# The S5 mixer of a four-layer backbone: chunks stored by step in the block, and the injection computed with tokens as the stationary side

## The chip, the cores and the metric

One core of a Trainium2 chip runs the whole program. The metric is the device time of one execution in microseconds (us); lower is better. The engines of the core are named as in the profile: PE (TensorE matmuls), PEld (its weight loads), DVE (VectorE), ACT (ScalarE), POOL (GpSimd) and SP, which only issues DMAs here. A difference of about 0.2% (4.4 us) is what a measurement of this kernel can tell from none.

## The reference

A backbone of four layers over 256 latent tokens and 256 context tokens of width 1024, all in float32. Each layer has a token mixer (latent attention, Hyena, S5, FNet, in that order) and a gated feed-forward part; both are normed and modulated. The change is in the S5 mixer of layer 2, cut here to what it computes:

```python
def s5_scan(u, lam_bar, b_bar, h0, reverse):
    bu = jnp.einsum('bngc,gsc->bngs', u.astype(jnp.complex64), b_bar)
    a = jnp.broadcast_to(lam_bar, bu.shape)
    a_cum, xs = lax.associative_scan(_lin_rec, (a, bu), axis=1, reverse=reverse)
    if h0 is None:
        return xs
    return xs + a_cum * h0[:, None]

# s5_mixer, for each direction (forward, backward), 64 groups of 16 channels, 64 complex states
xs_ctx = s5_scan(u_ctx, lam_bar, b_bar, None, reverse)
h0 = xs_ctx[:, 0] if reverse else xs_ctx[:, -1]
xs_lat = s5_scan(u_lat, lam_bar, b_bar, h0, reverse)
y_lat = y_lat + jnp.einsum('bngs,gcs->bngc', xs_lat, c_mat).real.reshape(B, L, D)
# after both: y = a * sigmoid(b) with (a, b) = gelu(y_lat) @ w_glu + b_glu
```

A linear recurrence runs over the context and then over the latent tokens, in either direction; only the latent tokens have an output.

## The kernel before

**How S5 is staged.** Each stream of 256 tokens is 32 chunks (`CH`) of 8 tokens (`STEP`), and 8 chunks are a block (`BLK`); context and latents together are 64 chunks, 8 blocks (`blocks`). The join that ends layer 1 writes the modulated tokens into `h_split` (L693) by step in the chunk, then chunk. 32 small DMAs (`tokens`, L2253; half from SP's queue, half from POOL's) bring them to `u`: partitions are 16 channels times 8 steps, and each of the 64 groups has 64 columns, its chunks.

**Injection.** `S5.tensor` has 16 rounds `n` (`NB`) of four groups. For every group and each of the real and imaginary parts (`i`) a matmul takes a 128x128 weight `et` as the stationary side and streams the group's 64 columns of `u` past it (L2475), into one bank; two banks (`INJECT`) alternate. ACT moves a bank into `e` with three copies (L2521 is a helper's line, that of every copy in `S5.scalar`): partitions 0 to 63 hold the states of the forward direction, 64 to 127 those of the backward one, which are written in reverse order. `e` is stored by group, part, step in the block and then block, so one step of all 8 blocks is 8 elements in a row.

**Recurrence.** On DVE, `inside` (L2375 to L2378) runs the seven steps within all blocks, four operations a step; `across` (L2385 to L2388) runs over the ends of the 8 blocks, 28 operations on 64 elements; `carries` (L2430 to L2433) adds to each step what the block before left. It is done for groups 0 to 31 (in two parts) and then 32 to 63. The `carries` of the first half run on POOL, those of the second on DVE, which waits for POOL first since both use `t0`.

**States to output.** `forward` and `backward` copy the states before each chunk from `e` to `s2` (on ACT, but for the second half's `backward`, which is DVE's). Meanwhile PE has computed the part within a chunk (L2489, weights `m0`). Then PE adds the states' part (L2502, weights `f`, once for each half), turns the result (L2513), and after the skip (L2412) and the Gelu comes the gated projection `Gated` (L864), whose result DVE multiplies (L2417).

**Order.** Every engine's program is written out by hand, stage after stage, and runs in order; semaphores join them. Two things are slotted in. The modulation vectors of later layers are computed in ticks (`mods`, L397: eight 32-row matmuls each, on 1 MB of weights that a `refill` on SP's queue brings, L360); `place` says how many ticks a stage does and how early the next loads may be issued. Every fourth tick ends a vector, which ACT copies (L408), PE turns (L374) and DVE stores (L418). SP issues in this order for S5: four `et` loads of 1 MB, the table of powers, two refills, the tokens, two refills, eight loads of `m0`, four more of `et`, eight of `f`.

## Time and profile before

| | us |
|---|---|
| time, median of 3 runs | 2223.07 |
| fastest and slowest of them | 2221.59, 2223.78 |
| the profiled execution's own time | 2222.09 |
| its span | 2220.3 |
| PE busy in it | 2089.5 (94%) |
| DVE, ACT, POOL busy | 1163.3, 865.4, 157.9 |
| S5's first injection matmul (L2475) starts at | 1547.08 |
| its last matmuls on the states (second L2502) start at | 1644.11 |

The page gives busy times and shares, the span in 40 slices, and the costliest groups. The 1.8 us between the span and the execution's time lie outside of the traced instructions. PE is busy nearly all of the time, so a stage matters by how long PE takes for it or is kept waiting in it. S5 stands at 1547 to 1716; in the page's 29th and 30th slice (each 55.5 us) the granted clock of PE falls to 0.5 and 0.7 of full speed, which is 2.4 GHz.

### The profile page before, as it was taken

The numbers are of one execution on the slowest core, as the hardware profiler recorded it, in microseconds if no ns is written. First come the engines' busy times: TensorE is split into PE (matmuls) and PEld (weight loads), VectorE is DVE, ScalarE is ACT, GpSimd is POOL, SyncE is SP. The second block draws the span as 40 slices with busy tenths as digits, with TensorE's granted clock in tenths as the row PEclk, the third lists the DMA queues.
The fourth block names the chain that finished last, engine by engine and source line by source line (L and its number), as shares of the span: only waits on it lengthen the run. The fifth ranks groups of instructions, "written<-read, shape, count | busy, mean of one in ns | idle before, by whom it ended". The sixth has DMA issues, their size and how long they took to land.

```text
span 2220.3 us, 31627 instructions
## 1 busy us (share of the span) xinstructions
PE 2089.5 (94%) x13233; PEld 1641.6 (74%) x13233; DVE 1163.3 (52%) x1961; ACT 865.4 (39%) x1416; POOL 157.9 (7%) x225
## 2 busy tenths in 40 slices
PE   4999999999999989999999999997959999898998
PEld 2756567777777767766468878875947899788997
DVE  2332552655666566647164665755661645526454
ACT  2442334433333453231253333344632544515444
POOL 0000110102101100010010210111200000000000
PEclk8999999999999999999999999998579999999999
DMA  6335341545535546442153443444584555314553
GB/s 258 133 111 183 133 152 42 197 147 172 178 119 187 180 172 216 165 135 103 57 170 106 130 136 100 141 134 162 233 305 145 190 189 175 123 58 153 189 184 102
DMA packets 227243, 342.14 MB, mean 154 GB/s; under 512 B 9590, under 2 KB 190625, under 8 KB 224860
## 3 DMA queue, kind: packets, MB, share of 16 engines
q1 hardware_dynamic: 216064, 310.27, 40.8%
q0 software_dynamic: 10320, 29.58, 4.6%
q8 instruction: 105, 1.72, 0.3%
q10 hardware_dynamic: 716, 0.26, 0.0%
q14 instruction: 38, 0.31, 0.0%
HBM read 317.66 MB, written 24.51 MB: 154 GB/s over the span
## 4 chain that ended last, share of the span: by engine, by line
PE 87%; DVE 7%; ACT 2%; DMA 2%; issue 1%; SPq 0%; POOL 0%; ACTq 0%; DVEq 0%
PE bank L956 21%; PE bank L957 20%; PE bank L958 20%; PE bank L819 4%; PE bank L397 3%; PE bank L864 3%; PE bank L2475 2%; PE bank L1724 1%; PE bank L1351 1%; PE bank L637 1%; DMA arena<-mod_w 1%; PE bank L2057 1%; PE bank L627 1%; PE bank L495 1%; DVE arena L710 1%; DVE arena L721 1%
## 5 line engine op out<-in xcount | busy, mean ns | idle before, releaser
L956 PE MATMUL bank<-h_hi,w_hi 128*128 128x512 f32 (+1 forms) x1480 | 512.0, 346 | 11.8 <-DVE h_lo L725 11.2
L957 PE MATMUL bank<-h_lo,w_hi 128*128 128x512 f32 (+1 forms) x1480 | 504.4, 341 | 0.0
L958 PE MATMUL bank<-h_hi,w_lo 128*128 128x512 f32 (+1 forms) x1480 | 504.4, 341 | 0.0
L917 DVE TENSOR_TENSOR w_lo<-ring,w_hi 128x1024 fp32r<-128x1024 f32 (+1 forms) x282 | 323.8, 1185 | 284.6 <-ACT w_hi L910 284.5
L956 PEld LDWEIGHTS bank<-h_hi,w_hi 128*128 128x128 f32 x1480 | 283.0, 191 | 50.8 <-DVE h_lo L725 15.3
L910 ACT ACTIVATE w_hi<-ring 128x1024 fp32r<-128x1024 f32 (+1 forms) x282 | 274.0, 1019 | 102.0 <-PE bank L958 100.2
L958 PEld LDWEIGHTS bank<-h_hi,w_lo 128*128 128x128 f32 x1480 | 283.0, 191 | 32.0 <-issue 0.2
L957 PEld LDWEIGHTS bank<-h_lo,w_hi 128*128 128x128 f32 x1480 | 283.3, 191 | 29.2 <-issue 0.2
L956 PE MATMUL bank<-g_hi,w_hi 128*128 128x512 f32 (+1 forms) x704 | 241.1, 342 | 0.0
L957 PE MATMUL bank<-g_lo,w_hi 128*128 128x512 f32 (+1 forms) x704 | 236.9, 337 | 0.0
L958 PE MATMUL bank<-g_hi,w_lo 128*128 128x512 f32 (+1 forms) x704 | 236.7, 336 | 0.0
L956 PEld LDWEIGHTS bank<-g_hi,w_hi 128*128 128x128 f32 x704 | 133.5, 190 | 22.7 <-issue 8.7
L958 PEld LDWEIGHTS bank<-g_hi,w_lo 128*128 128x128 f32 x704 | 133.5, 190 | 14.3
L957 PEld LDWEIGHTS bank<-g_lo,w_hi 128*128 128x128 f32 x704 | 133.6, 190 | 12.9
L1076 ACT ACTIVATE g_hi<-arena 128x512 fp32r<-128x512 f32 (+1 forms) x88 | 45.9, 525 | 234.4 <-DVE arena L1101 234.4
L1070 ACT ACTIVATE arena<-bank 128x512 f32<-128x512 f32 (+1 forms) x88 | 42.8, 491 | 190.3 <-PE bank L958 188.6
L397 PE MATMUL bank<-mod_ring,silu_c 128*32 128x256 f32 x1408 | 94.1, 392 | 24.2 <-DMA mod_ring<-mod_w 24.1
L1101 DVE TENSOR_TENSOR arena<-arena,bank 128x512 f32<-128x512 f32 (+1 forms) x88 | 48.2, 551 | 112.4 <-PE bank L958 110.5
L397 PEld LDWEIGHTS bank<-mod_ring,silu_c 128*32 128x32 f32 x1408 | 39.5, 111 | 63.7 <-DMA mod_ring<-mod_w 29.2
L956 PE MATMUL bank<-h_hi,hy_w_hi 128*128 128x512 f32 x192 | 76.4, 398 | 0.8 <-DVE h_lo L725 0.7
L957 PE MATMUL bank<-h_lo,hy_w_hi 128*128 128x512 f32 x192 | 74.9, 390 | 0.0
L958 PE MATMUL bank<-h_hi,hy_w_lo 128*128 128x512 f32 x192 | 74.8, 390 | 0.0
(328 smaller groups left out, 2959.7 us busy)
## 6 DMA issues: line engine op xcount, KB each, us to landing
ring<-ffn_w SPq DMA_DIRECT2D x120, 1024.0 KB, 5.1
mod_ring<-mod_w SPq DMA_DIRECT2D x88, 1024.0 KB, 6.8
ring<-ffn_w SPq DMA_DIRECT2D x16, 768.0 KB, 4.6
ring<-hy_w_in SPq DMA_DIRECT2D x12, 1024.0 KB, 5.3
arena<-mod_w SPq DMA_DIRECT2D x8, 1024.0 KB, 17.3
s_in_weights<-arena POOLq DMA_DIRECT2D x32, 256.0 KB, 3.3
s_out_weights<-arena POOLq DMA_DIRECT2D x16, 512.0 KB, 3.4
arena<-s_in_weights SPq DMA_DIRECT2D x8, 1024.0 KB, 10.9
```

The costliest lines, as they stand in the source:

```text
L397: last = nc.tensor.matmul(MODB[32 * g:32 * g + 32, 0:256], silu_c[:, k, :], self.slot(m)[:, kk, 256 * g:256 * g + 256], start=(k == 0), st ...
L819: last = nc.tensor.matmul(self.banks[c % 4][:, 0:self.n], v[:, kl, q * P:(q + 1) * P], self.rhs(k), start=(k == 0), stop=(k == self.kk - 1))
L864: last = nc.tensor.matmul(self.bank(c, t)[:, 0:self.n], v[:, k, q * P:(q + 1) * P], self.rhs(k), start=(k == 0), stop=(k == KD - 1))
L910: nc.scalar.activation(self.hi[:, i % SPLIT, a:b], self.w.slot(i)[:, a:b], ACT.Copy).then_inc(w_rounded, 1)
L917: last = unit.tensor_tensor(self.lo[:, i % SPLIT, c:c + w], self.w.slot(i)[:, c:c + w], self.hi[:, i % SPLIT, c:c + w].bitcast(F32), ALU.s ...
L956: nc.tensor.matmul(o, w[0], v[0], start=first, stop=False)
L957: nc.tensor.matmul(o, w[0], v[1], start=False, stop=False)
L958: return nc.tensor.matmul(o, w[1], v[0], start=False, stop=last)
L1070: nc.scalar.activation(self.silus[:, q, 0:n], self.out(i, q)[:, 0:n], ACT.Silu).then_inc(ffn_silu, 1)
L1076: nc.scalar.activation(g_hi[:, c + q, 0:n], self.silus[:, q, 0:n], ACT.Copy).then_inc(ffn_g_rounded, 1)
L1101: nc.vector.tensor_tensor(self.silus[:, q, 0:n], self.silus[:, q, 0:n], self.out(i, q)[:, 0:n], ALU.mult).then_inc(ffn_product, 1)
L2475: last = nc.tensor.matmul(bank[self.INJECT[n % 2]][:, o:o + 2 * CH], self.et[:, c % 4, 4 * (n % 2) + gb, i, :], self.u[:, 4 * n + gb, :], ...
```

## The change

**Layout.** The tokens are written to `h_split` with a chunk's place as step in the block first, then block, and with context and latents exchanged, so that context comes first. `e` becomes group, part, stream (context or latents, `a`), step in the block `q`, block `b` (four to a stream). One step of a stream is a run of four elements, and a group's part is a run of 64 in the order in which it leaves the bank. `ends` is a small area of its own for the ends of the blocks before each latent block.

**Injection.** A round has four matmuls: a group's 64 columns of `u` are the stationary side and the 256 columns of `et` (both parts) stream; two groups go to partitions 0 to 63 and 64 to 127 of the bank (`inject`). The bank is copied to SBUF (`move_injected`: DVE for rounds 0 to 3, ACT after), four PE transposes turn it so that states are partitions (`turn_states`, banks `STATES`), and ACT copies it to `e` with two copies. A round's turn is issued behind the next round's matmuls.

**Recurrence.** `across` of the first half moves from DVE to POOL, ahead of `carries`; each `carries` gets two small copies to `ends`. POOL now also waits until all rounds are in `e`.

**Queues and ticks.** The two refills ahead of the tokens on SP's queue are gone, the last four `et` loads come right behind the tokens, and two modulation ticks leave the join of layer 1; `states` has four in place of two, `scan` two in place of four, and the join in the middle of layer 3 has two in place of none. The multiplication at the end (L2417) becomes four operations a column block.

```diff
-                if self.fills:
+                if self.fills == 2:
                     mods.tensor(pe, (self, 1))
...
                         if self.split:
-                            src = src.rearrange("p (m s) -> p m s", s=STEP)
-                            dst = h_split[:, :, k, a // LAT, :].rearrange("p s m -> p m s")
+
+                            src = src.rearrange("p (b q s) -> p b q s", q=BLK, s=STEP)
+                            dst = h_split[:, :, k, 1 - a // LAT, :].rearrange("p s (q b) -> p b q s", q=BLK)
...
-            SCAN = [4 * (BLK - 1) * n + 4 * (2 * CH // BLK - 1) + c for n, c in ((2, 0), (1, 8))]
+            ACROSS, CARRIES = 4 * (2 * CH // BLK - 1), 10
+            SCAN = [4 * (BLK - 1) * 2, 4 * (BLK - 1) + ACROSS + CARRIES]
...
+                pool.wait_ge(self.e_moved, 2 * self.NB)
...
-                self.carries(nc.gpsimd, slice(0, 32), self.t0, self.raw.rearrange("p i s g -> p (i s g)"), then)
+                gs = slice(0, 32)
+                self.across(nc.gpsimd, gs, self.t0[:, 0:64], self.t0[:, 64:128], (self.signed[:, 0], self.signed[:, 1]), then)
+                self.carries(nc.gpsimd, gs, self.t0, self.raw.rearrange("p i s g -> p (i s g)"), then)
...
-                self.e = area(4096, GROUPS, 2, STEP, 2 * CH // BLK)
+                self.e = area(4096, 2 * GROUPS, 2 * CH).rearrange("p (g r) (a q b) -> p g r a q b", r=2, a=2, q=BLK)
...
+                self.ends = area(29184, GROUPS, 2, 4)
...
+                self.rows = self.t0.rearrange("p (a n) -> p a n", a=2)
...
-                mods.place((self, "turn"), 0)
-                mods.place((self, "states"), 2, p0 + 0.3)
-                mods.place((self, "scan"), 4, p0 + 0.4)
+                mods.place((self, "states"), 4, p0 + 0.4)
+                mods.place((self, "scan"), 2, p0 + 0.4)
                 mods.place((self, "turns"), 2, p0 + RING)
...
-                mods.refill(sp, p0 + 0.1)
                 for qt in range(4):
                     self.tokens(sp, 0, qt)
+                for c in range(4, 8):
+                    inject(c)
                 mods.refill(sp, p0 + 0.2)
...
                 for c in range(8):
                     toeplitz(c)
-                for c in range(4, 8):
-                    inject(c)
-                sp.wait_ge(self.e_summed, self.NB)
+                sp.wait_ge(self.e_summed, self.injected(self.NB - 1))
...
+                for n in range(2):
+                    self.move_injected(dve, V.tensor_copy, n)
...
+                for a in range(2):
+                    V.tensor_copy(self.signed[:, a], self.lab[:, 2 + a, 0:32]).then_inc(self.placed, 1)
+                for n in range(2, 4):
+                    self.move_injected(dve, V.tensor_copy, n)
...
-                    wide = lambda a: self.lab[:, a, gs].unsqueeze(3).to_broadcast([P, gs.stop - gs.start, 2, blocks])
-                    ta, tb = (v[:, 0:(gs.stop - gs.start) * 2 * blocks].rearrange("p (g r b) -> p g r b", r=2, b=blocks) for v in (self.scaled, self.t1))
+                    n = gs.stop - gs.start
+                    wide = lambda a: self.lab[:, a, gs].unsqueeze(3).unsqueeze(4).to_broadcast([P, n, 2, 2, blocks // 2])
+                    ta, tb = (v[:, 0:n * 2 * blocks].rearrange("p (g r a b) -> p g r a b", r=2, a=2, b=blocks // 2) for v in (self.scaled, self.t1))
                     for i in range(1, BLK):
-                        prev, cur = self.e[:, gs, :, i - 1, :], self.e[:, gs, :, i, :]
+                        prev, cur = self.e[:, gs, :, :, i - 1, :], self.e[:, gs, :, :, i, :]
                         scan(V.tensor_tensor(ta, wide(0), prev, ALU.mult), False)
...
-                        dve.wait_ge(self.e_moved, 3 * gs.stop // 4)
+                        dve.wait_ge(self.e_moved, 2 * gs.stop // 4)
...
-                        if gs.start == 0:
-                            mods.vector(dve, (self, "turn"))
-                    across(slice(32 * hf, 32 * hf + 32))
-                dve.wait_ge(self.carried, 8)
+                gs = slice(32, 64)
+                self.across(V, gs, self.scaled[:, 0:64], self.t1[:, 0:64], (self.lab[:, 2, gs], self.lab[:, 3, gs]), scan)
+                dve.wait_ge(self.carried, self.ACROSS + self.CARRIES)
...
+                    order = lambda v: v.rearrange("p (s q b) -> p b s q", s=STEP, q=BLK)
+                    dst = Y[:, c, 0:LAT].rearrange("p (b q s) -> p b s q", q=BLK, s=STEP)
+                    src, gate = order(self.up.bank(c, 0)[:, 0:LAT]), order(self.sig[:, c % 2, :])
+                    for b in range(CH // BLK):
+                        last = V.scalar_tensor_tensor(dst[:, b], src[:, b], vcol("s5_b_glu", c), gate[:, b], ALU.add, ALU.mult)
+                    last.then_inc(self.glu, 1)
...
+            def across(self, unit, gs, ta, tb, factors, scan):
+
+                ends = self.e[:, gs, :, :, BLK - 1, :]
+                ta, tb = (v.rearrange("p (g r) -> p g r", r=2) for v in (ta, tb))
+                for b in range(1, 2 * CH // BLK):
+                    prev, cur = ends[:, :, :, (b - 1) // 4, (b - 1) % 4], ends[:, :, :, b // 4, b % 4]
+                    scan(unit.tensor_tensor(ta, factors[0], prev, ALU.mult), False)
+                    scan(unit.tensor_tensor(tb[:, :, ::-1], factors[1], prev, ALU.mult))
+                    scan(unit.tensor_tensor(ta, ta, tb, ALU.add))
+                    scan(unit.tensor_tensor(cur, cur, ta, ALU.add))
...
+                scan(unit.tensor_copy(self.ends[:, gs, :, 0:1], self.e[:, gs, :, 0, nq, 3:4]), False)
+                scan(unit.tensor_copy(self.ends[:, gs, :, 1:4], self.e[:, gs, :, 1, nq, 0:3]))
                 tq = [self.tab[:, i, 0:nq, gs].rearrange("p q g -> p g q").unsqueeze(3).to_broadcast([P, n, nq, 4]) for i in range(2)]
-                end = [self.e[:, gs, r, nq, 3:7].unsqueeze(2).to_broadcast([P, n, nq, 4]) for r in range(2)]
+                end = [self.ends[:, gs, r, :].unsqueeze(2).to_broadcast([P, n, nq, 4]) for r in range(2)]
```
```diff
-                dst, src = self.states(slice(0, STATE), hf)
-                copy(dst[:, :, :, 0], src[:, :, 3:7, BLK - 1]).then_inc(done, 1)
-                copy(dst[:, :, :, 1:BLK], src[:, :, 4:8, 0:BLK - 1]).then_inc(done, 1)
+                dst, ends, src = self.states(slice(0, STATE), hf)
+                copy(dst[:, :, 0:4], ends).then_inc(done, 1)
+                copy(dst[:, :, 4:CH], src).then_inc(done, 1)
...
+            INJECT, STATES, OUT, TURNED = (0, 1), (4, 5), (0, 1, 4, 5), ((0, 1), (4, 5))
...
+                if n >= 2:
+                    pe.wait_ge(self.placed, self.moved(n - 2))
+                for p in range(2):
+                    for z in range(2):
+                        gb = 2 * p + z
+                        last = nc.tensor.matmul(bank[self.INJECT[n % 2]][64 * z:64 * z + 64, 256 * p:256 * p + 256], self.u[:, 4 * n + gb, :],
+                                                self.et[:, c % 4, 4 * (n % 2) + gb].rearrange("p i n -> p (i n)"), start=True, stop=True)
+                last.then_inc(self.e_summed, 1)
+
+            def move_injected(self, eng, copy, n):
+                eng.wait_ge(self.e_summed, self.injected(n))
+                if n >= 2:
+                    eng.wait_ge(self.e_summed, self.turned(n - 2))
+                copy(self.rows[:, n % 2], bank[self.INJECT[n % 2]][:, :]).then_inc(self.placed, 1)
+
+            def turn_states(self, pe, n):
+
+                pe.wait_ge(self.placed, self.moved(n))
+                if n >= 2:
+                    pe.wait_ge(self.e_moved, 2 * (n - 1))
+                dst = bank[self.STATES[n % 2]][:, :].rearrange("p (a z i j) -> p a i z j", a=2, z=2, i=2)
+                for p in range(2):
+                    for i in range(2):
+                        o = 256 * p + P * i
+                        last = nc.tensor.transpose(dst[:, p, i], self.rows[:, n % 2, o:o + P], ident[:, :])
+                last.then_inc(self.e_summed, 1)
...
+                for n in range(self.NB + 1):
+                    if n < self.NB:
+                        self.inject(pe, n)
+                    if n:
+                        self.turn_states(pe, n - 1)
...
-                    act.wait_ge(self.e_summed, n + 1)
-                    src = bank[self.INJECT[n % 2]][:, :].rearrange("p (g b q) -> p g b q", g=8, q=BLK)
-                    dst = self.e[:, 4 * n:4 * n + 4].rearrange("p g r q b -> p (g r) b q")
-
-                    copy(dst[0:STATE, :, 4:8], src[0:STATE, :, 0:4]).then_inc(self.e_moved, 1)
-                    copy(dst[0:STATE, :, 0:4], src[0:STATE, :, 4:8]).then_inc(self.e_moved, 1)
-                    copy(dst[STATE:P, :, ::-1, ::-1], src[STATE:P]).then_inc(self.e_moved, 1)
-                act.wait_ge(self.carried, 8)
+                    if n == 3:
+                        act.wait_ge(self.placed, self.moved(3))
+                    if 3 <= n < self.NB - 1:
+                        self.move_injected(act, copy, n + 1)
+                    act.wait_ge(self.e_summed, self.turned(n))
+
+                    src = bank[self.STATES[n % 2]][:, :].rearrange("p (a m) -> p a m", m=CH)
+                    dst = self.e[:, 4 * n:4 * n + 4].rearrange("p g r a q b -> p (g r a) (q b)")
+                    copy(dst[0:STATE], src[0:STATE]).then_inc(self.e_moved, 1)
+                    copy(dst[STATE:P, :, ::-1], src[STATE:P]).then_inc(self.e_moved, 1)
+                mods.scalar(act, (self, "states"))
+                act.wait_ge(self.carried, self.ACROSS + self.CARRIES)
...
-                for key in ("turn", "states", "scan"):
-                    mods.scalar(act, (self, key))
+                mods.scalar(act, (self, "scan"))
...
-            if l == 2:
-                mid.place_mods((2, 0))
+            else:
+                mid.place_mods((2,))
             ffn = Ffn(l, n_out, mid, post, TICKS[l])
             if l == 0:
                 post.place_mods()
             if l == 1:
-                post.place_mods((2, 2), (len(panels) + 0.1, len(panels) + 0.2))
+                post.place_mods((2, 0), (len(panels) + 0.2, None))
             if l == 2:
-                post.place_mods((2, 0))
+                post.place_mods((2,))
```

PE, between the join of layer 1 (L495 spreads its norms) and the gated projection; `bank` is PSUM, `arena` the large SBUF area. Before:

```order
L495 MATMUL bank<-r_post,sel 128x128 x4
L495 MATMUL bank<-r_pre,sel 128x128 x4
L397 MATMUL bank<-mod_ring,silu_c 32x256 x16
L2475 MATMUL bank<-arena 128x64 x64
L374 MATMUL bank<-ident,mod_rows 128x128 x2
L2475 MATMUL bank<-arena 128x64 x64
L2489 MATMUL bank<-arena 32x128 x64
L397 MATMUL bank<-mod_ring,silu_c 32x256 x16
L2502 MATMUL bank<-arena,tail 32x128 x64
L397 MATMUL bank<-mod_ring,silu_c 32x256 x16
L374 MATMUL bank<-ident,mod_rows 128x128 x2
```

Now, with `ring` holding the copied rows; the pair of four matmuls and four transposes stands 15 times, of which the rows show the first ones and the last:

```order
L495 MATMUL bank<-r_post,sel 128x128 x4
L495 MATMUL bank<-r_pre,sel 128x128 x4
L2505 MATMUL bank<-arena 64x256 x8
L2524 MATMUL bank<-ident,ring 128x2x64 x4
L2505 MATMUL bank<-arena 64x256 x4
...
L2524 MATMUL bank<-ident,ring 128x2x64 x8
L2542 MATMUL bank<-arena 32x128 x64
L397 MATMUL bank<-mod_ring,silu_c 32x256 x16
L374 MATMUL bank<-ident,mod_rows 128x128 x2
L397 MATMUL bank<-mod_ring,silu_c 32x256 x16
L2555 MATMUL bank<-arena,tail 32x128 x64
L397 MATMUL bank<-mod_ring,silu_c 32x256 x16
```

The 16 matmuls of ticks (L397) between L495 and the injection are gone, the 128 matmuls of 128x64 are 64 of 64x256 with 64 transposes between them, and the ticks stand behind L2542 (L2489 before). The line numbers are those of the changed kernel.

POOL, from its token DMAs on. Before:

```order
L2253 DMA arena<-h_sb 128x1x128 x16
L2430 TENSOR_TENSOR ring<-ring,arena 128x896
L2431 TENSOR_TENSOR ring<-ring,arena 128x896
L2432 TENSOR_TENSOR ring<-ring 128x896
L2433 TENSOR_TENSOR arena<-arena,ring 128x32x7x4
```

Now (the four operations on 64 elements stand seven times before the copies):

```order
L2256 DMA arena<-h_sb 128x1x128 x16
L2436 TENSOR_TENSOR ring<-ring,arena 128x64
L2437 TENSOR_TENSOR ring<-ring,arena 128x32x2
L2438 TENSOR_TENSOR ring<-ring 128x64
L2439 TENSOR_TENSOR arena<-arena,ring 128x64
...
L2444 COPY arena<-arena 128x64
L2445 COPY arena<-arena 128x64x3
L2451 TENSOR_TENSOR ring<-ring,arena 128x896
L2452 TENSOR_TENSOR ring<-ring,arena 128x896
L2453 TENSOR_TENSOR ring<-ring 128x896
L2454 TENSOR_TENSOR arena<-arena,ring 128x32x28
```

The 28 small operations of `across` and two copies stand ahead of the eight of `carries`.

## Rows read from the trace of the kernel before

**Rows 1.** The chain that ended last, in order of time: start us, us, what.

```profile
1537.35 9.69 DMA arena<-h_sb
1547.08 27.57 PE bank L2475 x128
1574.65 0.43 PE bank L374 x2
...
1604.69 0.70 DVE bank L2375
...
1624.12 0.27 DVE bank L2385
...
1631.43 1.09 DVE ring L2430
...
1640.20 3.82 ACT tail L2521 x2
1644.11 6.30 PE bank L2502 x128
1650.41 1.04 PE bank L2513 x8
...
1655.43 27.63 PE bank L864 x128
```

**Rows 2.** Groups by shape, 1545 to 1660 us; columns as in the page's part 5.

```profile
L2475 PEld LDWEIGHTS bank<-arena 128*128 128x128 f32 x256 | 54.8, 333 | 1.2 <-DMA arena<-h_sb 1.2
...
L2521 ACT ACTIVATE arena<-bank 64x512 f32<-64x512 f32 x16 | 17.9, 1116 | 0.4
...
L2521 ACT ACTIVATE tail<-arena 64x1792 f32<-64x1792 f32 x3 | 10.1, 3359 | 0.0
L2377 DVE TENSOR_TENSOR bank<-bank,ring 128x256 f32<-128x256 f32 x14 | 6.1, 432 | 0.5
...
L2521 ACT ACTIVATE arena<-bank 128x512 f32<-128x512 f32 x3 | 1.7, 584 | 2.8 <-PE bank L2502 2.8
```

**Rows 3.** Busy times by stretch; the last three are clock, DMA share, GB/s.

```profile
core 0: us, PE busy (x) PEld busy (x) DVE busy (x) ACT busy (x) POOL busy (x), PEclk, DMA share, GB/s
...
1566.00:1572.00 6.00, 6.00 (x30) 6.00 (x30) 5.62 (x15) 3.67 (x6) 0.00 (x0) 0.50 1.03 419
...
1606.00:1610.00 4.00, 3.03 (x80) 1.97 (x72) 3.85 (x6) 0.00 (x0) 3.92 (x3) 1.00 1.01 420
...
1630.00:1634.00 4.00, 1.51 (x18) 0.62 (x18) 3.79 (x9) 0.38 (x1) 0.00 (x0) 1.00 0.84 270
```

**Rows 4.** SP's queue in time: start us, us, what.

```profile
1526.65 1.25 SPq L360 DMA_DIRECT2D mod_ring<-mod_w  x2
```

**Rows 5.** PE in order of time, 1544 to 1630 us.

```profile
1544.87 1.94 PE L397 MATMUL bank<-mod_ring,silu_c 128*32 128x256 f32 x16 [3.69 <-DMA mod_ring<-mod_w]
...
1602.21 5.09 PE L2489 MATMUL bank<-arena 128*32 128x128 f32 x128
...
1622.06 5.40 PE L2502 MATMUL bank<-arena,tail 128*32 128x128 f32 x128 [13.03 <-ACT tail L2521]
```

**Rows 6.** DVE in order of time, the end of layer 1's join.

```profile
1543.49 0.69 DVE L721 TENSOR_TENSOR arena<-x_sb,bank 128x512 f32<-128x512 f32 x1
```

**Rows 7.** POOL in time, first and last of eight operations of `carries`.

```profile
1596.22 2.32 POOL L2430 TENSOR_TENSOR ring<-ring,arena 128x896 f32<-128x896 f32 x1 [46.24 <-DVE arena L2388]
...
1612.11 2.08 POOL L2433 TENSOR_TENSOR arena<-arena,ring 128x896 f32<-128x896 f32 x1
```

**Rows 8.** Groups by shape on POOL, the whole span.

```profile
L917 POOL TENSOR_TENSOR mla_o_lo<-ring,mla_o_hi 128x256 fp32r<-128x256 f32 x16 | 11.8, 771 | 247.2 <-ACT mla_o_hi L910 247.2
```

**Rows 9.** PE in order of time, between two shapes of tile, 1491 us.

```profile
1491.05 0.39 PE L958 MATMUL bank<-g_hi,w_lo 128*128 128x512 f32 x1
1491.36 0.43 PE L627 MATMUL bank<-arena,ones 128*32 128x128 f32 x8
```

**Rows 10.** All engines in order of time, the join inside layer 3.

```profile
2001.46 0.71 PE L495 MATMUL bank<-r_post,sel 64*128 64x128 f32 x4
...
2002.92 1.21 DVE L917 TENSOR_TENSOR w_lo<-ring,w_hi 128x1024 fp32r<-128x1024 f32 x1
```

84 lines of the change are left out of this document (34 added, 50 removed).

## The prediction

> **What bounds the kernel now.** I read the page first: PE is busy for 94% of the span, so the question for each stage is what PE does or waits for in it. Then the chain of waits through S5 [rows 1]. It goes through three things. PE's injection, two times 27.6 us for 64 matmuls each from 1547.08, with the turn of a modulation vector between them. Then DVE's recurrence on the second half of the groups, `inside` from 1604.69, `across` from 1624.12, `carries` from 1631.43. Then two ACT copies of 3.82 us at 1640.20, and PE's second run on the states at 1644.11. So 97.0 us lie between the first injection matmul and that run, and the injection is more than half of them.
>
> Why is the injection so slow? A matmul here takes 55.1/128 = 0.43 us for 64 columns (two records each, 0.215 us). The gated projection streams 256 columns with 0.216 us a record at the full clock [rows 1], which is about two cycles of 2.4 GHz a column, four for both records. The injection ran at half the clock, 0.50 [rows 3], and at 1.2 GHz four cycles for each of 64 columns would be 0.213 us, half of the measured 0.43. The other half is the weight load: PEld is busy for 54.8 us, as long as PE itself [rows 2]. PE was loading weights all the time.
>
> What stands ahead? The last tick before the injection waited 3.69 us for its weights and ran at 1544.87 [rows 5]; its 2 MB stand on SP's queue at 1526.65 [rows 4], ahead of the tokens, whose DMAs took 9.69 us [rows 1].
>
> **The start.** Two loads of 1 MB leave the head of the queue. At the 419 GB/s of a full stretch [rows 3] they are 2.1 MB / 419 = 5.0 us, and the ticks that waited for them are gone too. The first injection matmul can come at about 1542 in place of 1547. But the copy of its bank is DVE's now, and DVE's last work in the join begins at 1543.49 and takes 0.69 [rows 6]. So the start of the pipeline is DVE's, about 1544. DVE then does two copies (0.7 each, priced by its own operation on 512 elements in rows 6), the tables (16 operations) and two more, some 5.5 us; round 3 is turned after that and copied by ACT by 1553. That is an estimate; the bounds are 1552 and 1556.
>
> **A round of injection on PE.** Four matmuls stream 256 columns at four cycles, 4096 cycles in a row; if the two halves of the array, 64 columns of it each, work side by side, 2048: 1.71 us at 1.2 GHz, 0.85 at 2.4. No row shows tiles of 64. Tiles of 32 do overlap: 64 matmuls of 128 columns (L2489) would be 32768 cycles in a row, 13.7 us at 2.4 GHz, and took 5.09, part of it at the low clock [rows 5]. I take the overlap as given and keep its failure as a rival. Four transposes are 0.86 us at 1.2 GHz (0.43 for two of L374) and 0.52 at 2.4 (1.04 for eight) [rows 1]. A change of tile shape costs about 0.1: L627 starts 0.31 us behind the matmul ahead of it, and these follow each other by 0.23 [rows 9]; two changes a round, 0.2. PE's round is thus 2.8 us at the low clock and 1.6 at the high one.
>
> The Trainium skill, TensorEngine Tiling (Array Packing), Performance Considerations, names this very exchange of the sides for at most 64 streamed columns, with a gain of two; under Key Properties it says that a change of the tiling mode drains the engine. The 0.1 us above is what a row shows of that drain; without it the round would be 0.2 us shorter, and since ACT sets the pace below, the sum would be the same.
>
> **A round on ACT.** One copy of the bank, 128x512: 0.58. Two of 64x512. Before, such a copy with scattered reverse writing took 1.12, while a 128x512 one in longer runs took 0.58 [rows 2]. The forward copy is now contiguous, 0.55. The backward one is still reversed, so it lies between 0.55 and 1.12; I take nearly the upper end, 1.0, as its nearest row is the reversed one. The round is 2.1 us on ACT (bounds 1.7 and 2.3).
>
> **Which sets the pace** hangs on PE's clock. At 1.2 GHz throughout the old injection [rows 3], PE did stream only half of the time. L2489, which streams densely in narrow tiles, got the clock to 1.00 by the stretch from 1606, and it stayed at 1.00 in a stretch where PE was busy for 1.51 of 4 us [rows 3]. The new round streams for nearly all of PE's time. I take it that the clock rises and that ACT sets the pace at 2.1. Round 15 is in `e` at 1553 + 12 x 2.1 = 1578.2. DVE's two parts of the first half cost 4 operations x 14 x 0.43 = 24 us [rows 2], so they end at 1577 at the earliest: about a tie. Runs of four in place of eight I cost at nothing on DVE: `carries` has runs of four already and takes 1.09 for 896 elements [rows 1], against 0.70 for 512, about 1 ns an element for either.
>
> **POOL, the new link.** It starts at 1578.3. The 28 operations on 64 elements have no row. POOL takes 0.77 us for 256 elements [rows 8] and 2.08 for 896 [rows 7], so 2.05 ns an element and 0.25 fixed: 0.38, with 0.04 between two on the mean 0.42, or 11.8 in all (bounds: 0.3 and 0.6 each, 8.4 and 16.8). The two copies 1.2. `carries` as now, from 1596.22 to 1614.19, 18.0 [rows 7]. Sum 31.0, POOL ends at 1609.3. DVE in parallel: third part 19.4 and `across` 7.3 [rows 1] from 1578.3, ends at 1605.0 and now waits 4.3 us for POOL, since `carries` share `t0`; then 0.5 + 8.8 for `carries` and 2.2 for its state copy, 1620.8.
>
> **From POOL to the second run.** ACT, which waits for POOL, has four state copies. Before, the large one took 3.36 us for 1792 elements [rows 2]; now its runs are 28 long, and at the 0.58 us of 512 it is at most 2.0. I take 1.75 and 0.35 for the small one, 2.1 a pair, 4.2 for both: 1613.6 with 0.1 of latency. PE's first run on the states is 5.40 as now [rows 5]: 1619.0. Then the two `scan` ticks, 1.9 (one took 1.94 at the low clock [rows 5], so about half of that at the high one): 1620.9. ACT copies the finished vector ahead of its last state copies, since its order is fixed: 1621.4, and 2.1 more: 1623.5. PE's second run starts at 1623.7 in place of 1644.11: **20.4 us** gained. What is last there is this chain; DVE's would have allowed the run 2 to 3 us earlier. The other loads are hidden: at 2.5 us a megabyte, `m0` is there by about 1581 and `f` by 1601, against a first need of `f` at 1613.
>
> The second run took 6.30 from a low clock against 5.40 of the first [rows 1, 5]; now it follows within some 3 us of other matmuls, for which I count 1.5 us (bounds 0 and 2.9, since its 64 matmuls of 128 columns, four side by side, are 8192 cycles, 3.4 us at 2.4 GHz).
>
> **What it costs elsewhere.** The multiplication at the end is four small operations in place of one: only the last column block is exposed, 0.1. The join in layer 3 gets two ticks, 1.9 us of PE ahead of its spread at 2001.46; DVE needs that spread at the end of its weight operation, 2002.92 + 1.21 [rows 10], and 2001.46 + 1.9 + 0.7 is 2004.1, the same moment: 0.3. If that cover failed it would be 1.9. The ticks moved into `states` run while PE waits for the recurrence.
>
> Sum against the profiled execution of 2222.1: - 20.4 - 1.5 + 0.1 + 0.3 = **2200.6, say 2201**. That execution lies 1.0 under the median of 2223.07, well within what can be told.
>
> **Rivals.** First, **the clock stays low** in the injection. For it: the old injection never left 0.50. Against it: what L2489 did. A round is then 2.8, round 3 is in `e` at 1555 and round 15 at 1588.6; all behind it is 10.4 later: 2211, or 2212 without the gain of the second run. A sentence beside: the Trainium skill, TensorE: Matmul & The Clock Gate, Part 4, says that transposes do not count as busy for the clock, and by that rule a third of PE's round would not help to raise it; no row here shows transposes for long enough to tell.
>
> Second, **ACT or POOL is dearer**: copies at the scattered price (2.8 a round, 3.5 + 1.7 more behind POOL) or POOL operations at 0.6 (5.0 more). Either gives 2206 to 2214, taken as 2209. The Trainium skill, GPSIMD Engine Reference, section 7, asks half as much again for reads with a step of over 8 bytes, which these are; by it the 28 operations would cost some 1.8 us more, and the time would be 2203.
>
> Third, **slower**: the two tiles of 64 columns do not overlap and the clock stays low, so that the change of sides buys nothing: both stream 65536 cycles. A round is 3.41 + 0.86 + 0.2 = 4.5 us, round 15 comes at 1560 + 54 = 1614, 36 later than above: 2238 at the worst. The point from which it decides is a round of 2.1 + 21.5 / 12 = 3.9 us. Against it: tiles of 32 overlap. If they fail to overlap at the high clock, a round is 2.4 and the time 2205.
>
> Fourth, **the gain is hidden by something later**, such as loads of `f` or ticks that wait for weights: around 2222. For it: `f` for the second half may start only after L2489's matmuls, and two ticks of `states` are queued behind all of `f`. Against it: the estimate above leaves them 8 us or more.
>
> **How the numbers follow.** Chances: forecast 0.53, low clock 0.24, dearer ACT or POOL 0.13, slower 0.05, hidden 0.05. The forecast's own bounds are 2194 (DVE's tie at 1577, POOL at 0.3, 2.9 at the second run) and 2207. With the low clock and the dearer copies the range is 2194 to 2213. Faster by over 0.2% (below 2218.6) 0.90, within 0.2% 0.05, slower 0.05; 0.2% is about what a measurement of this kernel tells.
>
> **What would show it.** In the changed kernel's profile: the first injection matmul at 1541 to 1543; 64 matmuls of 256 columns whose pairs start together; the clock at 1.00 within some 8 us of the start, else the first rival; PE idle before a round for ACT, with a period of 2.1; DVE waiting for POOL by 4 us ahead of its `carries`; POOL's small operations at 0.38. I am wrong if the period is above 2.8, if POOL's chain is over 36 us, or if PE's second run starts after 1636.

## The result and the profile after

The changed kernel takes 2190.28 us (median of 4 runs, 2188.50 to 2190.54) against 2222.74 of the kernel before; the ratio is 0.9852, with a 95% interval of 0.9835 to 0.9869. It is faster by 32 us, where 22 were forecast (2201 against the 2223.07 known then): 2201 was 11 us too high, and the measured time lies below the range, which began at 2194. The profiled execution took 2190.54, its span is 2188.7 against 2220.3.

A difference of two traces needs a common mark. The sums of the join ahead of the mixer (the eight matmuls of L495 for `r_post`) start at 1529.26 us after and at 1527.39 before, though no stage up to there was changed. In the twelve other kernels of this study that start lies between 1526.73 and 1530.80, whatever was edited, so it differs by two microseconds either way from execution to execution. Below, "from the mark" means from that start, and a time "on the base of before" is one of the changed kernel less these 1.87 us. The granted clock too differs between executions in which nothing ahead was edited: the second run of state matmuls takes 3.70 us in some kernels of this study and 5.37 in others, behind the same idle 2.57 us of PE.

PE in order of time, from the end of layer 1's join to the gated projection (start us, us, what, idle before and its releaser; shortened), answering [rows 5] and the chain of [rows 1]:

```profile
1542.92 3.68 PE L2505 MATMUL bank<-arena 128*64 128x256 f32 x16 [9.70 <-DMA arena<-h_sb]
...
1609.89 5.03 PE L2555 MATMUL bank<-arena,tail 128*32 128x128 f32 x128 [2.49 <-ACT tail L2574]
1614.73 1.91 PE L397 MATMUL bank<-mod_ring,silu_c 128*32 128x256 f32 x32
1619.22 5.37 PE L2555 MATMUL bank<-arena,tail 128*32 128x128 f32 x128 [2.57 <-ACT tail L2574]
...
1629.75 27.79 PE L865 MATMUL bank<-arena,ring 128*128 128x256 f32 x128
```

The groups by shape, 1540 to 1660 us, answering [rows 2, 7]:

```profile
L2505 PE MATMUL bank<-arena 128*64 128x256 f32 x128 | 18.9, 423 | 9.7 <-DMA arena<-h_sb 9.7
L2574 ACT ACTIVATE arena<-bank 64x512 f32<-64x512 f32 x32 | 18.8, 587 | 1.8 <-PE bank L2524 1.4
L2524 PE MATMUL bank<-ident,ring 128*128 128x128 f32 x64 | 11.0, 296 | 1.5 <-ACT ring L2574 1.1 <-DVE ring L2513 0.2
...
L2505 PEld LDWEIGHTS bank<-arena 128*64 128x64 f32 x128 | 8.5, 147 | 15.6 <-DMA arena<-h_sb 10.1 <-issue 3.3 <-DVE bank L2374 0.2
L2574 ACT ACTIVATE ring<-bank 128x512 f32<-128x512 f32 x12 | 7.2, 597 | 0.3
...
L2390 DVE TENSOR_TENSOR bank<-bank,arena 128x256 f32<-128x256 f32 x14 | 6.0, 432 | 3.5 <-ACT arena L2574 3.1
L2574 ACT ACTIVATE tail<-arena 64x1792 f32<-64x1792 f32 x3 | 5.0, 1680 | 0.0
...
L2451 POOL TENSOR_TENSOR ring<-ring,arena 128x896 f32<-128x896 f32 x2 | 3.5, 1738 | 0.2
L2436 POOL TENSOR_TENSOR ring<-ring,arena 128x64 f32<-128x64 f32 x7 | 2.5, 351 | 28.6 <-DVE arena L2393 28.2
```

PE's weight loads fell from 54.8 us to 8.5, and 7.0 more for the transposes. At 64x512 a copy with long runs, forward or reversed, costs ACT 587 ns, where the scattered and reversed one took 1116; at 64x1792 it costs 1680 ns, where the scattered one took 3359 [rows 2].

Busy times by stretch, answering [rows 3]; the clock is the column behind POOL:

```profile
core 0: us, PE busy (x) PEld busy (x) DVE busy (x) ACT busy (x) POOL busy (x), PEclk, DMA share, GB/s
1542.00:1546.00 4.00, 3.08 (x16) 1.72 (x16) 3.97 (x8) 3.29 (x6) 2.21 (x6) 0.50 0.63 143
1546.00:1550.00 4.00, 3.90 (x26) 2.11 (x24) 3.93 (x22) 3.25 (x6) 2.97 (x7) 0.77 0.80 160
1550.00:1572.00 22.00, 20.65 (x154) 11.27 (x148) 17.88 (x44) 20.74 (x39) 0.18 (x1) 1.00 0.98 373
...
1596.00:1610.00 14.00, 3.98 (x36) 1.32 (x40) 12.18 (x37) 4.01 (x4) 9.45 (x5) 0.50 0.83 319
```

The clock rose from 0.50 to 1.00 within the first rounds of the injection and stayed there to its end: the forecast's branch, not the first rival's. (It is at 0.50 again from 1596 to 1610, where PE waits for the recurrence.)

GpSimd's line in time, answering [rows 7]: it waits for DVE's second part, not for ACT, whose last four copies, those of the last two rounds, start at 1571.90 and take 2.43:

```profile
1571.90 2.43 ACT L2574 ACTIVATE arena<-bank 64x512 f32<-64x512 f32 x4
```

```profile
1578.34 0.34 POOL L2436 TENSOR_TENSOR ring<-ring,arena 128x64 f32<-128x64 f32 x1 [28.15 <-DVE arena L2393]
...
1589.42 0.30 POOL L2444 COPY arena<-arena 128x64 f32<-128x64 f32 x1
1589.64 0.35 POOL L2445 COPY arena<-arena 128x192 f32<-128x192 f32 x1
1590.07 1.74 POOL L2451 TENSOR_TENSOR ring<-ring,arena 128x896 f32<-128x896 f32 x1
...
1603.59 2.10 POOL L2454 TENSOR_TENSOR arena<-arena,ring 128x896 f32<-128x896 f32 x1
```

**A stage that the sum left out.** The gain is not all in the mixer. The start of layer 3's channel DFT, PE in order of time, first the kernel before, then the changed one:

```profile
1933.57 0.71 PE L495 MATMUL bank<-r_pre,sel 64*128 64x128 f32 x4 [1.37 <-DVE r_pre L758]
1942.46 0.69 PE L374 MATMUL bank<-ident,mod_rows 128*128 128x128 f32 x2 [8.19 <-ACT mod_rows L408]
1942.95 8.81 PE L2595 MATMUL bank<-arena,h_sb 128*128 128x256 f32 x32
1951.59 1.67 PE L2604 MATMUL bank<-arena 128*128 128x256 f32 x7
```

```profile
1908.16 0.71 PE L495 MATMUL bank<-r_pre,sel 64*128 64x128 f32 x4 [1.37 <-DVE r_pre L759]
1910.17 5.12 PE L2651 MATMUL bank<-arena,h_sb 128*128 128x256 f32 x16 [1.30 <-ACT h_sb L694]
1916.76 3.72 PE L2651 MATMUL bank<-arena,h_sb 128*128 128x256 f32 x16 [1.47 <-DVE arena L2670]
1920.32 13.98 PE L2660 MATMUL bank<-arena 128*128 128x256 f32 x64
```

Before, the closing join of layer 2 had a second part, whose only content was the turn of the last vector (L374). PE waited 8.19 us in it for ACT's copy L408, which stands on ACT behind all eight shifted chunks (L693; the first ends at 1935.43), and only then began the DFT that could have followed the chunks one by one. ACT before:

```profile
1941.54 0.60 ACT L693 ACTIVATE h_sb<-arena,modv,affine 128x256 f32<-128x256 f32 x1 [0.19 <-DVE arena L721]
1942.05 0.36 ACT L408 ACTIVATE mod_rows<-bank 128x256 f32<-128x256 f32 x1
```

The diff's `post.place_mods((2,))` for layer 2 dropped that part. From the sums `r_pre` to the second transform it is 18.02 us before and 12.16 after: 5.9 us.

The 31.6 us between the spans, from the mark: the second run of state matmuls starts 116.72 us after it before and 89.96 now (-26.8); from there to the projection's first matmul (1655.27 and 1629.75 by the records; the chain of [rows 1] puts it 0.16 later) 11.16 and 10.53 (-0.6); from it to the next join's sums 66.23 and 65.72 (-0.5); from those sums to the second transform of layer 3 230.09 and 224.85 (-5.2: the 5.9, less 0.6 in the network of layer 2 that stands between, 212.07 and 212.69 up to the sums for `r_pre`; the turn moved into it, but as b_turn_out has 212.29 there and a_forward_first 212.16, it is not shown that the turn is what costs the 0.6); from there to the end -0.3; and +1.9 for the mark itself.

### The profile page after: what moved, and what is told of

Read it like the earlier page. It is cut to its first block, busy times and chain, and to the rows that moved or that the text cites. A ratio compares the mean times of both kernels' runs of the same rounds, so it can differ in the third digit from the quotient of the medians.

```text
span 2188.7 us, 31557 instructions
## 1 busy us (share of the span) xinstructions
PE 2064.7 (94%) x13169; PEld 1603.5 (73%) x13169; DVE 1160.8 (53%) x1965; ACT 848.8 (39%) x1412; POOL 165.7 (8%) x255
## 4 chain that ended last, share of the span: by engine, by line
PE 87%; DVE 6%; ACT 2%; DMA 2%; POOL 1%; issue 1%; SPq 0%; ACTq 0%; DVEq 0%; POOLq 0%
PE bank L957 21%; PE bank L958 21%; PE bank L959 21%; PE bank L820 4%; PE bank L397 4%; PE bank L865 3%; PE bank L1725 1%; PE bank L1352 1%; DMA arena<-mod_w 1%; PE bank L637 1%; PE bank L2058 1%; PE bank L627 1%; DVE arena L722 1%; DVE arena L711 1%; PE bank L495 1%
## 5 line engine op out<-in xcount | busy, mean ns | idle before, releaser
L397 PE MATMUL bank<-mod_ring,silu_c 128*32 128x256 f32 x1408 | 96.2, 397 | 18.3 <-DMA mod_ring<-mod_w 18.3
L397 PEld LDWEIGHTS bank<-mod_ring,silu_c 128*32 128x32 f32 x1408 | 40.6, 112 | 58.2 <-DMA mod_ring<-mod_w 22.3
```

What stands on the lines that cost most here:

```text
L397: last = nc.tensor.matmul(MODB[32 * g:32 * g + 32, 0:256], silu_c[:, k, :], self.slot(m)[:, kk, 256 * g:256 * g + 256], start=(k == 0), st ...
```

## Experiments

The theory: the mixer's gain is that of the forecast's chain (clock up, column tiles side by side, GpSimd as a new link), with DVE and not ACT setting GpSimd's start, and the rest is the turn in layer 2's closing join. Twelve kernels test it. Times are medians, and ratios are to the kernel before as it ran beside them (2221.9 to 2222.7; 2224.1, one run, beside the last three); "mixer" is the time from the mark to the projection's first matmul, 127.88 before and 100.49 after. Where nothing in it was edited it still varies, since the clock in the two state runs does: b_turn_out, whose mixer is that of before, has 126.26. In the kernels with the changed mixer the first of these runs takes 3.67 to 6.54 us and the second 3.70 or 5.37 (5.22 in a_across_dve). So a difference of 1.7 us between two traces of the mixer can be the clock alone, and starts ahead of these runs tell more than the sum.

| kernel | us | ratio, 95% interval | mixer, us |
|---|---|---|---|
| changed kernel | 2190.28 | 0.9852, 0.9835 to 0.9869 | 100.49 |
| b_turn_out | 2217.11 | 0.9976, 0.9967 to 0.9985 | 126.26 |
| a_turn_in | 2209.15 | 0.9941, 0.9928 to 0.9953 | 101.04 |
| a_early_ticks | 2194.59 | 0.9878, 0.9863 to 0.9892 | 106.78 |
| a_across_dve | 2193.34 | 0.9873, 0.9858 to 0.9888 | 104.90 |
| a_no_column_pairs | 2188.88 | 0.9854, 0.9837 to 0.9870 | 100.24 |
| a_act_slow | 2190.98 | 0.9856, 0.9840 to 0.9872 | 101.71 |
| a_parts_8_24 | 2188.68 | 0.9847, 0.9833 to 0.9860 | 99.76 |
| a_forward_first | 2189.45 | 0.9849, 0.9836 to 0.9863 | 98.48 |
| a_both | 2185.98 | 0.9841, 0.9826 to 0.9856 | 97.36 |
| a_left_thrice | 2211.14 | one run | 122.61 |
| a_ends_wide | 2192.32 | one run | 100.43 |
| a_ends_odd | 2193.14 | one run | 104.53 |

### The turn alone, out of the kernel before

```diff
             if l == 2:
-                post.place_mods((2, 0))
+                post.place_mods((2,))
```

with `fills` as the number of parts, as in the change.

> The kernel before, in which the join that closes layer 2 places its two ticks as one part and not as two, so that the turn of the last vector (its copy by ACT and its two transposes) leaves this join and goes to layer 3's feed-forward network; nothing else is changed. Theory: the turn held PE for the 8.19 us in which it waited for ACT's copy, which stands behind all eight shifted chunks, and the channel DFT of layer 3 could start only behind it. Without it the DFT follows the chunks one by one, and about 5.9 us of the 31.6 between the two kernels' spans come from here alone: 2222.7 - 5.9 = 2216.8, with the first DFT matmul 5 us or more earlier behind the join's sums and the mixer of layer 2 unchanged. Rival 1: the DFT is paced by the last chunk either way, so the turn's wait was covered, and the 5.9 us come from layer 2's mixer or from how layer 3's vectors are ready: 2222.7, no change. Rival 2: the turn costs as much where it goes to (the network's first panel waits for ACT): a gain of under 1 us, 2222.

Measured: 2217.11, 4.9 under before, with an interval of 3.3 to 7.3. PE in order of time:

```profile
1934.75 0.71 PE L495 MATMUL bank<-r_pre,sel 64*128 64x128 f32 x4 [1.37 <-DVE r_pre L758]
1936.76 0.67 PE L2595 MATMUL bank<-arena,h_sb 128*128 128x256 f32 x2 [1.30 <-ACT h_sb L693]
1937.60 4.98 PE L2595 MATMUL bank<-arena,h_sb 128*128 128x256 f32 x14 [0.17 <-ACT h_sb L693]
1943.35 3.72 PE L2595 MATMUL bank<-arena,h_sb 128*128 128x256 f32 x16 [0.77 <-DVE arena L2614]
1946.90 1.46 PE L2604 MATMUL bank<-arena 128*128 128x256 f32 x6
```

From `r_pre`'s sums to the second transform 12.15 us, where it was 18.02: the 5.9 us are there in a kernel whose mixer is the old one. Its mark came 1.2 us later, and from the mark its end is 6.0 us earlier than before. Both rivals fall, and the missing stage is shown.

### The turn, back into the changed kernel

```diff
-            else:
+            if l == 2:
                 mid.place_mods((2,))
...
-                post.place_mods((2,))
+                post.place_mods((4, 0))
```

> The changed kernel, in which the join that closes layer 2 again has two parts, (4, 0), and layer 3's middle join none: four ticks ahead of its spreads, and the turn of the last vector behind them. Theory: the turn waits for ACT's copy behind the eighth chunk and holds back the DFT: the changed kernel's 2190.3 + 5.9 = 2196.2, and up to 0.9 us more for two more ticks ahead of the spreads: 2196 to 2197. Rival: the stage's gain came with the storage of the tokens or with the mixer, and the place of the turn is worth nothing: 2190.3 to 2191.2.

Measured: 2209.15, some 19 us slower and not 6. PE in order of time:

```profile
1902.93 2.08 PE L397 MATMUL bank<-mod_ring,silu_c 128*32 128x256 f32 x30
1913.79 1.93 PE L397 MATMUL bank<-mod_ring,silu_c 128*32 128x256 f32 x16 [8.77 <-DMA mod_ring<-mod_w]
1916.20 1.94 PE L397 MATMUL bank<-mod_ring,silu_c 128*32 128x256 f32 x16 [0.48 <-DMA mod_ring<-mod_w]
...
1930.07 0.69 PE L374 MATMUL bank<-ident,mod_rows 128*128 128x128 f32 x2 [8.19 <-ACT mod_rows L408]
```

The turn's wait is back at 8.19 us, and from `r_pre`'s sums to the second transform it is 18.04 us again (1920.66 to 1938.70). The rest is mine: `mod_ring` holds the panels of two ticks, so a third tick in one place waits for a load that is issued only when the first has been used. That cost 13 us, which I had priced at 0.9. It was a bad dose, and b_turn_out is the clean test.

### The loads ahead of the tokens

```diff
-                post.place_mods((2, 0), (len(panels) + 0.2, None))
+                post.place_mods((2, 2), (len(panels) + 0.1, len(panels) + 0.2))
...
-                mods.place((self, "states"), 4, p0 + 0.4)
+                mods.place((self, "states"), 2, p0 + 0.3)
...
+                mods.refill(sp, p0 + 0.1)
                 for qt in range(4):
                     self.tokens(sp, 0, qt)
```

> The changed kernel, in which the join that closes layer 1 has its two later ticks again, with their 2 MB ahead of the tokens on SP's queue (and the place ahead of the state matmuls two fewer, where they were hidden). Theory: the ticks wait for their weights and the tokens come behind them, as before: the first injection matmul at 1547 to 1549 in place of 1542.9. DVE is busy with the join until 1546 in either, so only part of it counts: the recurrence starts 4 to 5 us later and the time is 2194 to 2196. Rival 1: the injection's speed has slack of 4 us against DVE at the end of the first half, but DVE's first part waits for four rounds, so no slack helps there: 2196 in full. Rival 2: the start is hidden, since DVE's tables take the same time: 2190.3.

Measured: 2194.59. The last tick waits 3.49 us for its panel, the first injection matmul starts at 1546.73, 5.4 us later from the mark, GpSimd 5.3 later and the projection 6.3. The early start is worth 4 to 6 us, as the forecast had it (5.0); of the 6.3, 0.9 is a first state run of 5.97 us at a lower clock in place of 5.03.

### `across` of the first half, back to DVE

```diff
-                self.across(nc.gpsimd, gs, self.t0[:, 0:64], self.t0[:, 64:128], (self.signed[:, 0], self.signed[:, 1]), then)
...
                         inside(gs)
-                gs = slice(32, 64)
-                self.across(V, gs, ...)
+                    gs = slice(32 * hf, 32 * hf + 32)
+                    self.across(V, gs, self.scaled[:, 0:64], self.t1[:, 0:64], (self.lab[:, 2, gs], self.lab[:, 3, gs]), scan)
```

> The changed kernel, in which the 28 small operations across blocks of the first half are DVE's again, as before the change; GpSimd has only the carries. Theory: DVE is the longer of the two lines then. It does them in 28 x 0.26 = 7.3 us, GpSimd's carries start at 1585.7 and end at 1602.0 (3.7 earlier), but DVE's third part ends 7.3 later and its carries end at 1621.6 in place of 1614.95, so the second run starts at 1623.7 in place of 1619.22: 4.5 slower, 2194.8. So the moved operations gave 4.5 of the 26.8 us. Rival 1: GpSimd's line (ACT's state copies and PE's first run behind it) sets the second run, and a faster across helps: up to 3.7 less, 2187. Rival 2: the two lines balance: within 1 us of 2190.

Measured: 2193.34. GpSimd starts its `carries` 3.6 us earlier from the mark and is through earlier, PE's first state run starts at 1604.07, and then the other line, DVE's, is late:

```profile
1604.07 3.67 PE L2554 MATMUL bank<-arena,tail 128*32 128x128 f32 x128
...
1621.24 5.22 PE L2554 MATMUL bank<-arena,tail 128*32 128x128 f32 x128 [7.72 <-ACT tail L2573]
```

The second run starts 94.5 us from the mark in place of 90.0, so 4.5 later, as expected; 3 to 4 of it reach the end. Moving the chain of small operations to GpSimd balanced two lines. In the changed kernel PE is through with the first run and the ticks at 1616.65, and DVE with its carries at 1614.95.

### The pace of the rounds, on PE

Order of the four matmuls of a round:

```diff
-                for p in range(2):
-                    for z in range(2):
+                for z in range(2):
+                    for p in range(2):
```

> The changed kernel, in which the four matmuls of an injection round come in the order left, left, right, right (column tiles of 64) instead of left, right, left, right. Theory: two tiles of 64 columns work side by side only where they follow each other, and DVE, not the injection, sets when the recurrence's second link starts. Then a round is 3 x 0.43 + 0.16 + 0.59 = 2.0 us on PE where it was 1.60, the period 2.0 and no longer ACT's 1.72, the last states are in place 12 x 0.3 = 3.6 us later, at 1577.9, just inside DVE's 1578.2, and the time stays 2190.3 (up to 1 us more, since the first four rounds are later by 0.5). Rival 1: the order is indifferent, the halves overlap anyway: a period of 1.72 and no change at all. Rival 2: nothing overlaps in this order: 4 x 0.43 + 0.75 = 2.46 a round, 9 us later at the end: 1583.3, and 5 us slower, 2195.

Measured: 2188.88, and PE's round is 1.61 us where it was 1.60. My theory that two tiles overlap only where they follow each other in turn falls; four matmuls in the order left, left, right, right overlap as well. Then the dose that tells side by side from a doubled rate:

```diff
-                    for z in range(2):
+                    for z in (0, 0, 0, 1):
```

> The changed kernel, in which each left matmul of an injection round (column tile 0 to 63) is issued three times in a row and the right one once, eight matmuls in place of four; the repeats write the same values, and the result is unchanged. Theory: two halves of the array work side by side, each at its own rate of 0.43 us for a matmul of 256 columns in its two passes. Then the left half has six of them, 2.56 us, and the round on PE is 2.56 + 0.75 = 3.3 us. Rival: a matmul on 64 columns of the array simply streams at twice the rate, whichever half it uses, 0.25 us each as the 1.01 us of a round of four allow: 8 x 0.25 + 0.75 = 2.8 us. Either way PE and no longer ACT (1.72) sets the pace, the last states come 12 x 1.6 = 19 or 12 x 1.1 = 13 us later, and DVE's slack of 4 takes some of it: 2205 or 2199.

PE in order of time:

```profile
1553.33 2.80 PE L2505 MATMUL bank<-arena 128*64 128x256 f32 x16
1556.07 0.66 PE L2524 MATMUL bank<-ident,ring 128*128 128x128 f32 x4
1556.65 2.80 PE L2505 MATMUL bank<-arena 128*64 128x256 f32 x16
```

A round takes 3.32 us, the 3.3 of two halves that work side by side (six times 0.43 on the left one), not 2.8. The time of 2211 is above the 2205 expected, because I had counted 12 slower rounds and all 16 were: the first two took 8.31 us for their matmuls at the low clock, where two at the full clock take 5.6. From the mark, ACT's last copy ends 26.5 us later and GpSimd starts 22.5 later, released by ACT here and not by DVE:

```profile
1599.12 0.35 POOL L2436 TENSOR_TENSOR ring<-ring,arena 128x64 f32<-128x64 f32 x1 [50.69 <-ACT arena L2574]
```

So DVE's slack saved the 4 us that it was counted at, and beyond it the pace of the rounds passes on in full.

### The pace of the rounds, on ACT

```diff
-                    copy(dst[0:STATE], src[0:STATE]).then_inc(self.e_moved, 1)
-                    copy(dst[STATE:P, :, ::-1], src[STATE:P]).then_inc(self.e_moved, 1)
+                    for rows, way in ((slice(0, STATE), 1), (slice(STATE, P), -1)):
+                        copy(dst[rows, 0:8, ::way], src[rows, 0:8])
+                        copy(dst[rows, 8:16, ::way], src[rows, 8:16]).then_inc(self.e_moved, 1)
```

> The changed kernel, in which each of ACT's two copies of a round (64x512, 587 ns) is cut into two of 64x256, so that a round costs ACT about 0.33 us more (two more starts of 0.15 to 0.17 each, from 587 ns at 512 and 1680 ns at 1792 elements) and its pace is the 2.05 to 2.1 us of the prediction in place of 1.71. Theory: the misjudged pace was worth little, since DVE's operations on the first half set GpSimd's start. Round 3 comes 1.2 us later and with it DVE; the last copies come 5 us later, at 1579.5, as late as DVE's new end, 1579.4. So GpSimd and all behind it are 1.2 to 1.5 us later: 2191.7. Rival: the pace passes on in full, 5.2 us, since DVE's parts wait for their rounds: 2195.5. If the first is right, the miss of 5.7 us in the end of the rounds made only some 1.5 us of the miss in the time.

Measured: 2190.98. The dose came out smaller than meant: a round takes 1.83 us and not 2.05, because the starts of neighbouring copies overlap (four of 370 ns in 1.31 us). From the mark, ACT's last copy ends 1.6 us later, GpSimd starts 0.3 us later. So a fifth of ACT's delay passed on (the mixer is 1.2 us longer, but 0.9 of it is the first state run, 5.94 us at a lower clock in place of 5.03). It speaks for the theory. A pace of the full 2.1 was not run; by the slack of 4 us in a_left_thrice, last copies that came 5.7 us later would have moved GpSimd by 1.7.

### The pace of the rounds, on DVE

```diff
-            PARTS = ((slice(0, 16), slice(16, 32)), (slice(32, 64),))
+            PARTS = ((slice(0, 8), slice(8, 32)), (slice(32, 64),))
```

> The changed kernel, in which DVE's first half is cut as 8 and 24 groups of states and not as 16 and 16. Theory: DVE, and not ACT's pace, sets when GpSimd may start: its 56 operations of 432 ns in two parts start only at 1554.28, when four rounds are in place, after an idle 3.09 us, and end at 1578.2, while ACT is done at 1574.33. With two rounds in the first part it starts at about 1551.3; the parts take 28 x 0.30 and 28 x 0.56 us (from 0.43 at 256 and 0.70 at 512 elements), 24.1 as before, and end near 1575.4. GpSimd and all behind it come 2.9 us earlier: 2187.4. Rival 1: ACT's rounds bound the start: it is 1574.33 against 1578.3 in any case, but with the second part's own wait (24 groups are in place with the eighth round at 1561) DVE stands idle there and the gain is 1 us or less: 2189.5 to 2190.3. Rival 2: the third part on DVE becomes the end (it waited 0.93 us for GpSimd) and keeps its time: 2190.3.

Measured: 2188.68. DVE's recurrence starts at 1550.68, right behind its own copies, and GpSimd starts 47.69 us from the mark in place of 49.08, so 1.4 us of the 2.9 came. Groups by shape on DVE:

```profile
L2390 DVE TENSOR_TENSOR bank<-bank,arena 128x384 f32<-128x384 f32 x7 | 4.0, 566 | 2.0 <-ACT arena L2574 1.8
```

DVE's work cost what I had said (566 ns at 384 elements), but between its parts it waits 1.8 us for round 7. I had named that wait as a rival and left it out of the theory's time; the gain (1.6 us in the time; 0.7 in the mixer, where a first state run of 5.70 us at a lower clock hides another 0.7) lies between the two. DVE bounds the start of GpSimd; ACT's last copy ends 2.7 us before it.

### ACT's order behind the first run

```diff
-                mods.scalar(act, (self, "scan"))
                 act.wait_ge(self.step, sum(self.SCAN))
                 self.forward(act, copy, 1, self.s_moved)
+                mods.scalar(act, (self, "scan"))
```

> The changed kernel, in which ACT issues the second half's forward state copies ahead of the copy of the 'scan' ticks' vector. Theory: the second run of state matmuls starts at the later of PE's own line (first run and ticks, 1616.65 in the changed kernel's trace) and ACT's copies, which can start when DVE's carries end (1614.95) and take 2.00; in the changed kernel they stand behind a copy that waits for the ticks until 1616.71. So the second run starts at 1617.05 and not at 1619.22: 2.1 us less, 2188.2. Rival 1: the copy's place is free, because DVE's own state copies (1614.98 to 1616.28) and the shared reads slow ACT's copies: under 0.5 us, 2190. Rival 2: the turn behind the mixer then waits for the delayed copy and gives the gain back: 2190.3.

Measured: 2189.45, 0.8 less and not 2.1, which by the times alone can't be told from nothing. PE in order of time:

```profile
1617.11 3.70 PE L2555 MATMUL bank<-arena,tail 128*32 128x128 f32 x128 [0.30 <-issue]
...
1624.82 1.07 PE L397 MATMUL bank<-mod_ring,silu_c 128*32 128x256 f32 x16 [1.76 <-DMA mod_ring<-mod_w]
1625.82 1.09 PE L2566 MATMUL bank<-ident,arena 128*128 128x128 f32 x8
1627.84 12.35 PE L865 MATMUL bank<-arena,ring 128*128 128x256 f32 x56 [0.92 <-DMA ring<-s_w_glu]
```

The second run starts at 1617.11, the 1617.05 of the theory, 2.2 us earlier from the mark, and takes 3.70 us instead of 5.37; that is 3.9 us by its end. The 1.7 of the clock are not shown to be the edit's, since a_no_column_pairs, a_left_thrice and a_ends_wide have 3.70 too, with PE's wait as it was. Two waits for loads then take 2 of the 3.9 back, and the ticks of the next join, which took 3.62 us in place of 2.08 at a granted clock of 0.57, another 1.5. A first edit that removes a wait shows the next one, here the loads.

Both edits together:

> The changed kernel with both small edits of before: DVE's first half cut as 8 and 24 groups, and ACT's last state copies ahead of the vector's copy. Theory: the first moves GpSimd's start by 1.3 us (DVE now waits 1.8 us for the eighth round between its parts), the second the second run of state matmuls by 2.1 more; but of such a gain the loads take some back, since the ticks behind the second run waited 1.76 us and the gated projection 0.92 us for weights as soon as the run came earlier, and SP can issue those only when DVE and PE are through with the buffers: the projection 2.5 to 3 us earlier than in the changed kernel, 2187.5. Rival 1: the sum of both in full, 3.4 us: 2186.9. Rival 2: a lower granted clock in the stages behind (the ticks of the next join took 3.62 us in place of 2.08 in the second edit alone) takes it all: 2189 to 2190.

Measured: 2185.98, below the theory's 2187.5 and rival 1's 2186.9. From the mark the projection starts 3.1 us earlier than in the changed kernel, and the next join's sums 3.0; the clock did not fall in that join here. The intervals of the two ratios overlap, but its four runs (2185.72 to 2188.32) all lie below the changed kernel's four (2188.50 to 2190.54). In the traces the second run starts 3.5 us earlier from the mark and is 1.7 shorter by the clock, of which the loads take 2.0 back. It is the fastest of the kernels here.

### Why the carries were cheaper

The ends of the blocks in unused slots of the states, 512 bytes from group to group; first aligned, then in the place of the kernel before:

```diff
-                self.ends = area(29184, GROUPS, 2, 4)
+                self.ends = self.e[:, :, :, 0, 0, :]
```

```diff
-                self.ends = area(29184, GROUPS, 2, 4)
+                self.ends = self.e[:, :, :, 0].rearrange("p g r q b -> p g r (q b)")[:, :, :, 3:7]
```

> The changed kernel, in which the ends of the blocks lie in unused slots of the states themselves, in runs of four, aligned at 16 bytes, one group 512 bytes from the next (in the changed kernel 32 bytes). GpSimd's two multiplications of the carries took 2341 and 2324 ns before the change, where they read the ends at an odd place with the step of 512 bytes, and 1738 ns after it. Theory: it is the step between groups that costs: 2.3 us again for each of four operations, 2.4 us later, 2192.7. Rival: it is where a run of four begins: 1738 ns stays, 2190.3.

> As the run before, but the runs of four begin at the fourth element, 12 bytes behind a border of 32, as in the kernel before the change. Theory of the step: 2.3 us for each multiplication. Rival, the place where the run begins: 2.3 us too here, and not in the run before. If both runs stay at 1.74, something else in the old layout cost the 0.6 us (the two operations run beside other work of DVE), and both kernels take 2190.3.

GpSimd's groups, first wide, then wide and odd:

```profile
L2451 POOL TENSOR_TENSOR ring<-ring,arena 128x896 f32<-128x896 f32 x2 | 3.5, 1736 | 0.2
```

```profile
L2451 POOL TENSOR_TENSOR ring<-ring,arena 128x896 f32<-128x896 f32 x2 | 4.6, 2319 | 0.2
```

The step between groups costs nothing; the place where a run of four begins costs 0.58 us for 896 elements. The times alone would have misled: a_ends_wide took 2192.32, nearly the 2192.7 of the theory of the step, but the kernel before took 2224.08 beside it, its mark is the latest of all (1530.80), and its mixer is as long as the changed kernel's. (a_ends_odd is 4.0 us longer in the mixer, 2.3 of them the four multiplications and 1.0 a first state run at a lower clock.) My theory of the step falls, and the rival holds: the separate `ends` gained by their alignment.

## Where the prediction was right and where it failed

**Right.** The injection was bound by weight loads and by the half clock, and exchanging the sides cured both; how its gain (55 us before, 30 now with the transposes) divides between the two no run here separates. The first injection matmul (1542.92; 1541.1 on the time base of before, forecast 1541 to 1543), PE's round (1.60, forecast 1.6), the tiles of 64 columns side by side (a_left_thrice), round 3 in place at 1554.2 (1552.4 on that base, forecast 1553), GpSimd's small operations (0.32 to 0.38 each, forecast 0.38), the state copies (4.03, forecast 4.2), the first state run (5.03, forecast 5.4), and the early start's 5 us (a_early_ticks). The rival of the low clock did not come. Nor did the price of half as much again for far reads that stands beside the second rival: GpSimd's operations on 64 elements took 0.32 us with all operands in a row and 0.35 to 0.37 with one of them at a step of 256 bytes, a tenth more. (The 1.8 us counted for it there would also make 2202.4 and not 2203.) A sentence beside it: the Trainium skill, TensorE: Matmul & The Clock Gate, Part 4, has transposes not counting as busy for the clock; here the clock rose to 1.00 and stayed there while PE spent 11.0 us in transposes beside 18.9 in matmuls, so they did not keep it down, and whether they helped no run here tells.

**Step that failed first: what lies outside the mixer.** The prediction's part on costs elsewhere priced the join in layer 3 (+0.3; measured at nothing, the end comes 0.3 earlier) and said nothing of layer 2's closing join, whose second part the diff removes as well. That is 5.2 of the 10.1 us between 2200.6 and 2190.54. The trace of before showed it, as a wait of 8.19 us for an ACT copy; I had followed the change's rows only around the mixer. b_turn_out shows it alone. Without this stage the time would have been some 2195.5, inside the range.

**Second: "A round on ACT", 2.1 us.** I took 1.0 for the reversed copy because its nearest row was reversed and scattered at once. The scatter is what had cost 1116 ns; reversed with long runs is 577 to 593, the same as forward. The round is 1.71, and ACT's last copies end at 1572.5 on the base of before, not at 1578.2. But it was worth little, because the sum had two terms in a tie there: with ACT's 1578.2 gone, DVE's parts, forecast at 1577, are the last, and they end at 1576.5. So GpSimd starts there and not at 1578.3, 1.8 us earlier. a_act_slow, a_parts_8_24 and the slack of 4 us in a_left_thrice show DVE as the bound.

**Third: "POOL, the new link", 31.0 us.** It was 27.35: the 28 operations 11.1 (forecast 11.8), two copies 0.65 (1.2), `carries` 15.6. I had carried over 18.0 for `carries` as it was, though the change gives it a new operand; aligned ends took 2.3 us from it (four multiplications of 0.58). With this link 3.65 shorter, DVE waited 0.93 us for GpSimd ahead of its own `carries`, where the forecast had 4.3. With the 0.9 by which the rest up to the second run was shorter, 1.8 + 3.65 + 0.9 makes the 6.4 us by which that run is earlier than forecast.

**Fourth, "the second run", 1.5 us.** The two traces give 0.9 (6.30 to 5.37), but the same run takes 5.21 us in b_turn_out, whose mixer is the old one. In the kernels with the changed mixer it is 5.37 or 3.70 behind the same wait of 2.6 us. So the gain that I had hung on the shorter wait is the granted clock of one execution or another, and what the change itself gave there is open.

In numbers: 6.4 (up to the second run) - 0.9 (from there to the projection 0.6 gained, where 1.5 was forecast) + 0.6 (up to the next join 0.5 gained, where 0.1 was a cost) + 5.2 (up to layer 3's second transform) + 0.6 (0.3 gained where 0.3 was a cost) - 1.9 (the mark) = 10.0, and the forecast's 2200.6 lies 10.1 above the profiled execution. The range held the uncertainties of one stage and none for the part of the diff that had not been priced, and that no bound of its terms could mend.

## What to carry to other kernels

Price every hunk of a diff, and for a place that goes away read what the engines waited for in it, however far from the main change: a wait of PE for a copy that stands at the end of ACT's queue holds back work that was long ready. When two lines tie, an error in one of them is worth only what the other allows, and an edit shows its gain only until the next wait, here for loads. Price an operation by its access pattern (runs, where they begin), not by its name.

## What the chip showed beyond that

- ACT: in these copies the price hangs on the length of the runs, not on the direction: 64x512 in 587 ns forward or reversed, 1116 scattered; 64x1792 in 1680 against 3359.
- GpSimd: a multiplication of 896 elements whose operand comes in runs of four (16 bytes) takes 1736 to 1738 ns where they begin at a multiple of 16 bytes and 2319 where they begin 12 bytes behind one; the step from run to run, 32 or 512 bytes, changes nothing. Its operation on 64 elements takes 0.32 to 0.38 us, DVE's 0.23 to 0.27.
- PE: matmuls on two column tiles of 64 overlap in either order of the four, and at full clock 16 records of them, three to one, take 2.80 us, where eight, two to two, take 1.08.
